# A two-layer decoder with mixture-of-experts: expert weight tiles cut another way, a nine-place ring used in turn, expert groups written out, and attention's first tiles asked for before the overflow check

## What is computed

```python
def expert_block(args):
    xk, e = args
    hid = jax.nn.silu(xk @ w_gate[e]) * (xk @ w_up[e])
    return hid @ w_down[e]
```

## Time and profile before

| | |
|---|---|
| time, median of 3 runs | 1554.23 us (1553.99 to 1555.08) |
| span of the profiled execution | 1553.8 us |
| PE busy | 1203.0 us (77%) |
| weight loads (queue q1) | 480.55 MB |
| mean rate over the span | 315 GB/s |

### The profile page before, as it was taken

How to read it: one execution, slowest core, us unless ns; L and a number is a source line. 1 busy time by engine, 2 the same in 40 slices (tenths; PEclk the granted TensorE clock), 3 DMA queues, 4 the chain that set the end, 5 groups by cost and what they waited for, 6 DMA issues and landing times.

```text
span 1553.8 us, 16438 instructions
## 1 busy us (share of the span) xinstructions
PE 1203.0 (77%) x6686; PEld 690.6 (44%) x6686; DVE 454.2 (29%) x881; ACT 394.7 (25%) x620; POOL 24.7 (2%) x39
## 2 busy tenths in 40 slices
PE   4999997867757667575999997977867777677676
PEld 4986775313313223132888885656313133133131
DVE  5744534100100100104766554745100100001001
ACT  4334422101101011013665633532101011011010
POOL 2000000000000000000000001100000000000000
PEclk9999996968888889898999998997978677687786
DMA  8542476999999999999454554676899999999997
GB/s 299 204 172 109 162 291 255 369 410 410 410 409 410 409 410 410 410 409 393 141 186 163 173 206 60 90 247 254 331 410 409 410 410 410 410 410 410 410 410 297
DMA packets 138567, 489.24 MB, mean 315 GB/s; under 512 B 5104, under 2 KB 5168, under 8 KB 138016
## 3 DMA queue, kind: packets, MB, share of 16 engines
q1 hardware_dynamic: 135888, 480.55, 79.1%
q0 software_dynamic: 2640, 8.15, 3.3%
HBM read 487.56 MB, written 1.12 MB: 314 GB/s over the span
## 4 chain that ended last, share of the span: by engine, by line
PE 45%; DMA 43%; DVE 4%; SPq 4%; ACT 2%; issue 1%; POOL 0%; ACTq 0%; POOLq 0%; DVEq 0%
DMA ring_more<-in_exp_down 21%; DMA ring<-in_exp_up 15%; PE triple L315 7%; PE triple L317 6%; PE triple L316 6%; PE triple L991 4%; SPq L755 4%; PE bank L958 4%; DMA ring<-in_exp_gate 3%; PE triple L1005 3%; PE bank L1005 2%; PE bank L317 2%; PE bank L315 2%; PE bank L316 2%; PE bank L1022 2%; DMA xT<-bias_rows 2%
## 5 line engine op out<-in xcount | busy, mean ns | idle before, releaser
L991 PE MATMUL triple<-ring,work 128*32 128x512 f32 x1536 | 234.5, 748 | 131.4 <-DMA ring<-in_exp_up 127.3
L991 PEld LDWEIGHTS triple<-ring,work 128*32 128x32 f32 x1536 | 49.0, 124 | 308.2 <-DMA ring<-in_exp_up 199.1
L1005 PE MATMUL triple<-ring_more,work 128*32 128x512 f32 x512 | 96.3, 832 | 111.7 <-DMA ring_more<-in_exp_down 105.7
L296 DVE TENSOR_TENSOR ring_lo<-ring,ring_hi 128x2048 fp32r<-128x2048 f32 x72 | 161.8, 2288 | 45.8 <-ACT ring_hi L289 45.7
L1096 DVE TENSOR_TENSOR work<-work,triple 128x512 f32<-128x512 f32 x16 | 11.0, 689 | 535.7 <-PE triple L991 535.7
L289 ACT CAST ring_hi<-ring 128x2048 fp32r<-128x2048 f32 x72 | 133.8, 1907 | 92.3 <-PE bank L317 49.2
L958 PE MATMUL bank<-work,hn 128*128 128x128 f32 x512 | 126.3, 419 | 15.4 <-DVE h L1105 10.9
L958 PEld LDWEIGHTS bank<-work,hn 128*128 128x128 f32 x512 | 123.3, 335 | 27.2 <-DVE h L1105 22.5
L1105 DVE TENSOR_TENSOR h<-h,bank 128x512 f32<-128x512 f32 x64 | 44.0, 688 | 294.3 <-PE bank L1022 294.3
L1005 PE MATMUL bank<-ring_more,work 128*32 128x512 f32 x512 | 98.7, 851 | 0.0
L315 PE MATMUL triple<-ring_hi,x_hi 128*128 128x512 f32 x240 | 95.3, 397 | 2.5 <-DVE work L656 1.5
(11 more groups left out here) (250 smaller groups left out, 1521.3 us busy)
## 6 DMA issues: line engine op xcount, KB each, us to landing
ring<-in_exp_up SPq DMA_DIRECT2D x64, 2048.0 KB, 23.8
ring_more<-in_exp_down SPq DMA_DIRECT2D x64, 2048.0 KB, 23.5
ring_more<-in_exp_gate SPq DMA_DIRECT2D x32, 2048.0 KB, 12.0
ring<-in_exp_gate SPq DMA_DIRECT2D x32, 2048.0 KB, 19.5
ring<-in_ret_w_in SPq DMA_DIRECT2D x12, 2048.0 KB, 8.8
ring<-in_w_kv SPq DMA_DIRECT2D x12, 2048.0 KB, 8.7
ring<-in_dil_wq SPq DMA_DIRECT2D x6, 2048.0 KB, 17.7
ring<-in_ret_w_out SPq DMA_DIRECT2D x4, 2048.0 KB, 7.9
```

Of the source, the lines that this page charges most:

```text
L296: nc.vector.tensor_tensor(ring_lo[:, dense_slot(n), cols], ring[:, dense_slot(n), cols], ring_hi[:, d % 2, cols].bitcast(F32), ALU.subtrac ...
L991: last = nc.tensor.matmul(bank[2 + kind][rows, :], m_x[:, k, rows], w[:, e, kk * FF:(kk + 1) * FF], start=(k == 0), stop=(k == KD - 1))
L1005: last = nc.tensor.matmul(bank[4 + nh][rows, :], m_hidT[:, k * P + e * SLOTS:k * P + (e + 1) * SLOTS], w[:, e, nh * 512:(nh + 1) * 512], s ...
```

## The change

1. **Tile shape.** A tile now holds half the rows of two experts, 8 KB in one run, instead of a quarter of the rows of four. Tiles 0, 1 of a matrix kind are experts 0-1 and 2-3 in the first half of the rows, tiles 2, 3 the same in the second half.
2. **Ring.** The 96 tiles of a layer go round all nine places in turn (`MOE_ORDER`), so each tile waits for the one nine before it. The first nine are issued in the order `FIRST_LOADS`, which again takes places 6, 7, 0, 1, 2, 3 first.
3. **PE's order.** PE works on a half (two tiles, 16 products) at a time and needs both tiles to begin; it gives each of them back at its last product, the 14th and the 16th. In down each output half takes its eight products one after the other.
4. **No loops.** The eight groups of a layer are written out for every engine; waits are on constants.
5. **Overflow.** The overflow check of layer 0 stands behind attention's first four tiles, and overflow weights go to places 6 to 8.

```diff
-MOE_SLOT = (6, 7, 0, 1, 2, 3, 4, 5, 8, 6, 7, 8)
+MOE_ORDER = (0, 1, 6, 7, 8, 5, 4, 2, 3)
+FIRST_LOADS = (2, 3, 0, 1, 7, 8, 5, 6, 4)
+OVER_SLOT = 6
...
+            def load(n):
+
+                it, j = n // MOE_TILES, n % MOE_TILES
+                kind = ("gate", "up", "down")[j // PER_GROUP]
+                half, pair = j % PER_GROUP // 2, it * PER_GROUP + j % 2 * 2
+                at = moe_at(n)
+                sp.dma_start(slot(at).rearrange("p (e c) -> p e c", e=2),
+                             rows[kind][:, pair:pair + 2, half * TILE // 2:(half + 1) * TILE // 2]
+                             ).then_inc(s_ring[at], 16)
...
-            with sp.Fori(1, EXPERT_GROUPS) as it:
-                for j in range(MOE_TILES):
-                    sp.wait_ge(s_used, it * MOE_TILES + (first + last_user(j) + 1))
-                    load(j, it * PER_GROUP)
-
+            for n in range(RING, TILES):
+                sp.wait_ge(s_used, first + n - RING + 1)
+                load(n)
...
+            def used(last, e, half):
+
+                if over:
+                    if half == 1:
+                        last.then_inc(s["used"], 1)
+                elif e % 2 == 1:
                     last.then_inc(s_used, 1)
...
-            with engine.Fori(0, EXPERT_GROUPS) as it:
+            for it in range(EXPERT_GROUPS):
                 group(engine, layer, it, PER_GROUP, m[layer]["main"], False)
...
-            overflow = moe_sp(sp, 0)
-            sp.wait_ge(m[0]["over"]["used"], 3 * overflow + 1)
+            moe_sp(sp, 0)
             for i in range(3 * N_KV):
...
+                if i == DENSE_RING:
+                    overflow = overflow_sp(sp, 0)
+                    sp.wait_ge(m[0]["over"]["used"], 3 * overflow + 1)
                 load_tile(sp, FIRST_QKV + i, src, KD)
```

More of the change, by code:

```diff
@@ L279, in split_act @@
             if n >= FIRST_QKV:
-                loads += MOE_SLOT.count(dense_slot(n)) * EXPERT_GROUPS
+                loads += moe_loads(dense_slot(n))
             if 0 in parts:
@@ L731, in build, with moe_rows @@
             })
[L733 to L743, removed]
+        def moe_rows(layer):
+            return {"gate": exp_gate[layer].rearrange("e (p k) f -> p e (k f)", k=KD),
+                    "up": exp_up[layer].rearrange("e (p k) f -> p e (k f)", k=KD),
+                    "down": exp_down[layer].rearrange("e (p k) n -> p e (k n)", k=FF // P)}
@@ L745, in moe_sp @@
         def moe_sp(sp, layer):
             first = FIRST_MOE[layer]
[L747 to L757, removed]
@@ L766, in moe_sp @@
+            for n in FIRST_LOADS:
+                at = moe_at(n)
+                if at in (6, 7):
+                    if layer == 0:
+                        sp.wait_ge(s_used, FIRST_WOUT + 1)
+                    else:
+                        sp.wait_ge(a_sc, 2 * DIL_H)
                 elif at < DENSE_RING:
@@ L779, in moe_sp @@
             with sp.If(count > 0):
-                sp.wait_ge(s_used, first + tiles)
+                sp.wait_ge(s_used, FIRST_MOE[layer] + TILES)
                 with sp.Fori(0, count) as b:
@@ L999, in group_pe @@
             pe.wait_ge(s["hidT_ready"], it + 1)
[L1000 to L1001 removed]
+            for half in range(2):
+                w = weights(2, half)
                 for nh in range(2):
[L1003 to L1008 removed]
+                    for kk in range(2):
+                        k = 2 * half + kk
+                        for e in range(experts):
+                            rows = slice(e * SLOTS, (e + 1) * SLOTS)
+                            last = nc.tensor.matmul(bank[4 + nh][rows, :],
+                                                    m_hidT[:, k * P + e * SLOTS:k * P + (e + 1) * SLOTS],
+                                                    w[e][:, kk * D + nh * 512:kk * D + (nh + 1) * 512],
+                                                    start=(k == 0), stop=(k == 3))
+                            if kk == 1 and nh == 1:
+                                used(last, e, half)
+                    if half == 1 and nh == 0:
                         last.then_inc(s["y_done"], 1)
[L1010 removed]
             pe.wait_ge(s["gselT_ready"], it + 1)
```

81 lines of the change are left out of this document (38 added, 43 removed).

## The result

| | before | after |
|---|---|---|
| median | 1554.3 us (1553.99 to 1555.08, 4 runs) | 1530.92 us (1525.68 to 1536.12, 4 runs) |
| ratio, 95% interval | | 0.9847 [0.983, 0.9864] |
| span of the profiled execution | 1553.8 us | 1534.2 us |

The change makes the kernel 23.4 us (1.5%) faster. The prediction said 1533.6 us, with 1523 to 1547 as its range.

The account below looks back on a forecast made before the run. The prediction took the weight stream as the bound. Layer 0's -10.4, layer 1's -11.2 and bias +1 made -20.6 on 1553.8, or 1533.2 us; the median standing 0.4 higher gave 1533.6 us, range 1523 to 1547.

Parts of the forecast that it names:

- packets: Expert weight stream: an 8 KB packet takes 311 ns, so each tile takes 0.14 us less, 11.8 us a layer.
- the stream's stop closed: Start of each layer's expert stream: refills no longer wait on tile 8, a down tile; 3.5 and 5.0 us gained.
- fetches: Written-out groups: 14 more instruction fetches a layer share the DMA engines with the weights, costing 2 us a layer.
- products behind the last tile: End of each layer's experts: 16 products instead of eight, 3.6 us more at the low clock, 0 at the high.
- ACT's slack: End of layer 0: normalization no longer waits behind the split of the first attention tile, giving back 0.7 us.
- bias load: Last bias load, met by layer 1's first tiles: its packets may wait behind 8 KB instead of 4 KB, +1 us.
- What bounds the kernel: Expert stretches: the stream of weights sets the pace, with DMA share 1.03 at 410 GB/s and PE waiting.
- The rule of the Trainium skill: Packet cost, rival of half the gain: 0.06 us a tile saved in place of 0.14, 1547 us, chance 0.06.
- all on one: Extreme of the rival that fetches gather on few DMA engines: 17.5 us a layer, 1565 us; whole rival's chance 0.12.
- PE keeps up: Expert groups: PE needs 59.0 us at 1.2 GHz against 59.8 us of stream; rival that PE becomes the bound, 0.05.

Follow-up runs that it names:

- after with 4 KB: Changed kernel with tiles cut as before, a quarter of the rows of four experts in 4 KB runs: 1558.42 us, ratio 1.0018.
- before written out: Kernel before with its expert groups written out for all engines in place of loops, nothing else changed: 1561.24 us, ratio 1.0033.
- tail: Changed kernel with the second half of each layer's last group taking its two down tiles one after the other: 1525.58 us, ratio 0.9822.
- tile-by-tile kernel: Changed kernel with PE waiting for one tile at a time and giving it back after its eight products: 1527.09 us, ratio 0.9817.

## Why the prediction was right

The streams' difference splits exactly, by the kernels in the first table, into packets (after less after with 4 KB), ring (that less before written out) and fetches (that less before):

| us | predicted, layers 0 and 1 | measured |
|---|---|---|
| packets | -11.8, -11.8 | -12.9, -13.2 |
| the stream's stop closed | -3.5, -5.0 | -3.7, -4.4 |
| fetches | +2, +2 | +1.7, +3.9 |
| products behind the last tile | +3.6, +3.6 | +4.6, +2.4 |
| ACT's slack | -0.7 | -0.1 |
| bias load | +1 | 0 |

- **What bounds the kernel: right.** DMA share 1 and PE's waits named the stream, and only what made the stream shorter or uncovered its ends moved the time.
- **The packet: right.** 311 ns was read off the line through 2, 4 and 16 KB, and 311 was measured. The rule of the Trainium skill ("DMA: Bandwidth & Descriptors", section "Why small descriptors are slow") would have given, as an estimate, 0.06 us a tile. The runs show 0.14 by the packets' durations and 0.15 by the streams, so the fixed part of 9.6 ns from the earlier trace rows is the one that holds at 8 KB too.
- **The stop in the stream: right.** SP issued its first refill 3.7 us after PE's start where 3.1 was expected, so 1.7 us later than before and not 1.3. The prediction counted 14 products at 0.22 us; why the 14th is given back 0.6 us after that, no run shows. The refills follow one another without another stop like that of the earlier trace rows.
- **Fetches: right together within 2 us**, the only term that no row had priced. Layer 1 paid twice what layer 0 did, and the landings show the difference: before, the engines were 1.8 us apart at the end of layer 0 and 0.3 at the end of layer 1, afterwards 3.4 and 3.6. That they were struck in this measure and not evenly or all on one is what the prediction could only choose between, so the size was a guess that held. The Trainium skill ("Runtime: NRT & Kernel Launch", section "Instruction fetch mechanics") gives stalls at taken branches as a reason to unroll, where a branch's target lies outside what is loaded. That case did not arise here: layer 1's loop ran without a fetch, and the kernel with loops was 6.1 us faster than the same kernel written out.
- **The last products: the two together near (7.0 against 7.2), by luck, for each by itself is off; in the changed kernel's second profile they are +3.8 and +1.6, 5.4 together.** In layer 0 the kernel before had found the 2.4 GHz level and done its eight in 1.9 us; the prediction had that row and still took the low-clock surplus. After, the granted clock was 0.54 over the 6.5 us (the line stands under "Tail" above), so the surplus was 4.6. In layer 1 both kernels began at 0.50, and after the change the clock rose to 0.82 for the last 1.7 us, so it was 2.4.
- **ACT's slack: wrong.** The step said that ACT stood behind the split of attention's first tile and would start 0.7 us earlier once the additions come last. The chain of work of the changed kernel (start, duration, what), here and, in its last line, for the next point:

```profile
713.08 0.70 DVE h L1127
713.77 0.02 issue
713.79 0.28 ACTq L1142
...
714.43 1.15 ACT hn L351 x2
...
999.49 10.24 DMA xT<-bias_rows
```

  Between the end of the last addition and the normalization there are still 0.66 us, where it was 0.73: some 0.5 us of it is ACT's own read of the overflow count (L1142, the line at which the change shows SP's read of `blocks`). Only 0.1 us went.
- **The bias load: wrong.** The load on the chain took 10.24 us, against 10.21 in the earlier trace rows, and 9.79 in the second profile. Packets twice as long in front of it did not make it longer. The stretch between the layers was 2.6 us longer in the profiled execution, but 365.5 us, 0.4 less than before, in the same kernel's second profile; among the kernels of the first table it goes from 365.5 to 368.5, and the same kernel stands at both ends. This variation, with that of the start, is most of the difference between the two spans of the changed kernel (1534.2 and 1527.6). What makes it was not tried.
- **PE keeps up: right.** The stretch of the earlier trace rows became 63% busy at clock 0.85.

The errors partly cancel in the sum: 20.6 predicted, 19.6 in the profiled spans, 23.4 in the medians, 25.2 when both kernels were run once more (1529.22 against 1554.37). The nearness of 19.6 is luck too, since that execution was the slowest of four. Streams and tails alone, which the change acts on, were predicted at -20.9 and came to -21.6 and -22.5 in the two profiles. What the prediction had right is how the gain comes about: packets first, then the closed stop, less fetches and a longer tail.

## What to carry to other kernels

Where DMA share is 1 and the engines wait, price the stream by the time of one packet at each size that the trace holds: the line through them gave the gain of longer runs to about 0.01 us a tile (0.14 against 0.15), and the rest of a large rewrite, together, was worth nothing. Then look at what stands behind the last byte and at which clock it runs: work that can be done before the last tile lands should be done before. A wait for two tiles in place of one cost 1.7 us at a layer's first refill and up to 3 us at its end. Written-out loops are not free when the DMA engines are saturated: each fetch delays one engine, and the tile waits for the latest.

## What the runs showed of the hardware

- Products that use 32 of the 128 columns took 0.11 us a record when they went round four strips at the 2.4 GHz level, and 0.22 within a run of eight or sixteen that stayed on two. A busy PE at full clock can therefore be at half its pace; in the tile-by-tile kernel PE was busy 1302.0 us in place of 1190.0, with the same work.
- A duration alone does not tell the two apart: 3.6 us for eight products is four strips at 1.2 GHz in one kernel and two strips at 2.4 GHz in the other. The column of the granted clock (0.50 and 1.00) has to be read beside it.
- Packets of 2, 4, 8 and 16 KB took 85, 160, 311 and 615 ns of a DMA engine: 387, 410, 421 and 426 GB/s on 16 engines.
- A 16 KB instruction fetch held one DMA engine for 0.9 to 1.4 us, and 26 more of them came with a kernel 6.1 us slower and with the landings of a layer's last tile 3.4 to 3.6 us apart, where it was 1.8 and 0.3.
- After a wait of 3.5 to 4.8 us for the last pair of tiles, PE's work ran at a mean granted clock of 0.54 to 0.68; in "tail", after waits of 1.1 and 1.0 us, it ran at 1.00, and in the kernel before, after 1.8 and 1.5 us, at 1.00 and 0.50.
